# Both gated MLPs' up projections as seven block products per slab, with GpSimd making sums and low parts

## The chip, the cores and the metric

One core of a Trainium2 chip runs the kernel in one launch. The metric is the device time of an execution in microseconds (us). The kernel before takes 1741.75 us, median of 3 runs (1741.56 to 1744.15).

## The reference

Two blocks run one after the other on a sequence of 512 tokens and 1024 channels, in float32. The first has two layers, each a token mixer and a gated MLP; the second has a recurrent and attention mixer and a plain MLP. The change touches the gated MLP of the first block's two layers:

```
def conv_ffn(h, w_up, conv_w, conv_b, w_down):      # h = rms_norm(x, norm2_g), 512 x 1024
    up = h @ w_up                                   # 512 x 5632
    conv = conv_b + padded[:, 0:s_len] * conv_w[0] + ...   # causal, width 3, per channel
    gate, val = jnp.split(conv, 2, axis=-1)         # 2816 each
    return (jax.nn.silu(gate) * val) @ w_down
```

## The kernel before

Every large product is made of three TensorE products in the type fp32r: an operand is split in a high part (ScalarE rounds it, `xh`, `wh`, `ah`) and a low part (the rest, VectorE subtracts, `xl`, `wl`, `al`), and `product` (L573 to L575) issues high x high, high x low, low x high. Weights come as slabs of 128 x 2048 floats (1 MB) in a fixed order through a ring of 3 slots. SyncE loads slab n+3 once TensorE signals `slab_used` for slab n; ScalarE's `high` (L1158) rounds it into `wh`; VectorE's `low_slab` (L1873) writes the rest over the raw slab; `slab_split` tells TensorE. Each engine follows one order written out by hand, with semaphores between them.

A gated MLP works in 11 groups j of 256 gate and 256 value channels: two up slabs and one down slab each. `up` multiplies an up slab with all 8 tiles of x (channels x 512 tokens) into two PSUM banks, 48 products of 512 columns. The tokens aren't normalised before: `scale_up` (L2073) multiplies the result by 1/rms into `upb`. ScalarE makes the first convolution tap (`conv_tap`, L1387), VectorE the other two (`conv_middle` L2079, `conv_first` L2086), ScalarE SiLU (L1397), VectorE the product (`gate`, L2098), ScalarE its high part (L1406), VectorE its low part (`gate_low`, L2103). `down` of group j-1 follows on TensorE behind `up` of group j: 8 output groups o, each 6 products of 512 columns, through 3 banks; VectorE's `add_down` (L2116) adds each to x (layer 0) or to the turned copy `yt` (layer 1), and output group o waits for the add of o-3. In between VectorE multiplies and sums one adaLN slab of the second block per group (`ada_sum`, L1861), which ScalarE's queue loads (L1349). TensorE's order in the loop, two groups per pass:

```
up(j, n, (MLP0 + 2) % RING)
down(it * 2 + v, v, n + 2, (MLP0 + 4) % RING)
```

GpSimd makes the low part of three slabs in the second block (`low`, L558), and nothing else.

## Time and profile before

| | us |
|---|---|
| median of 3 runs | 1741.75 |
| profiled execution | 1741.62 |
| its span, first to last instruction | 1739.8 |
| TensorE busy | 1724.3 (99%) |
| VectorE busy | 1266.6 (73%) |
| ScalarE busy | 769.2 (44%) |
| GpSimd busy | 14.0 (1%) |

In the profile PE is TensorE's matmuls, PEld its weight loads, DVE VectorE, ACT ScalarE, POOL GpSimd, SP SyncE. L573 is line 573 of the kernel. The granted TensorE clock is 0.999 of full speed on average. Durations of matmuls include their way through the array, so they overlap; the distance between two starts is what one costs.

### The profile page before, as it was taken

The numbers are of one execution on the slowest core, as the hardware profiler recorded it, in microseconds if no ns is written. First come the engines' busy times: TensorE is split into PE (matmuls) and PEld (weight loads), VectorE is DVE, ScalarE is ACT, GpSimd is POOL, SyncE is SP. The second block draws the span as 40 slices with busy tenths as digits, with TensorE's granted clock in tenths as the row PEclk, the third lists the DMA queues.
The fourth block names the chain that finished last, engine by engine and source line by source line (L and its number), as shares of the span: only waits on it lengthen the run. The fifth ranks groups of instructions, "written<-read, shape, count | busy, mean of one in ns | idle before, by whom it ended". The sixth has DMA issues, their size and how long they took to land.

```text
span 1739.8 us, 22776 instructions
## 1 busy us (share of the span) xinstructions
PE 1724.3 (99%) x8652; PEld 1403.2 (81%) x8652; DVE 1266.6 (73%) x1788; ACT 769.2 (44%) x1053; POOL 14.0 (1%) x7
## 2 busy tenths in 40 slices
PE   9999999999999999999999999999999999999998
PEld 8896888888888989688888888888766788888886
DVE  6377786776777646878678688766589568777778
ACT  6424442333333523344233233355798474454442
POOL 0000000000000000000000000000000200000000
PEclk9999999999999999999999999999999999999999
DMA  8330334333333233043433433353410233222321
GB/s 291 122 119 27 121 121 145 121 121 132 134 121 121 97 99 120 25 144 110 145 121 121 145 121 121 121 175 122 120 37 2 73 100 112 104 97 97 113 105 49
DMA packets 33352, 195.27 MB, mean 112 GB/s; under 512 B 5760, under 2 KB 7168, under 8 KB 11264
## 3 DMA queue, kind: packets, MB, share of 16 engines
q1 hardware_dynamic: 24656, 156.77, 26.3%
q10 hardware_dynamic: 8624, 37.49, 6.6%
q8 instruction: 50, 0.82, 0.2%
q14 instruction: 22, 0.18, 0.0%
HBM read 187.43 MB, written 2.11 MB: 109 GB/s over the span
## 4 chain that ended last, share of the span: by engine, by line
PE 94%; DVE 3%; issue 1%; ACT 1%; DMA 1%; SPq 0%; DVEq 0%; ACTq 0%; PEldq 0%
PE ps L573 29%; PE ps L574 29%; PE ps L575 29%; PE ps L714 1%; PE ps L728 1%; PE ps L974 1%; PE ps L956 1%; PE ps L992 1%; PE ps L631 1%; DMA raw<-in_weights 1%; DVE acc L2612 1%; PE ps L736 0%; PE ps L892 0%; DMA x<-in_xin 0%; DVE pb L2396 0%
## 5 line engine op out<-in xcount | busy, mean ns | idle before, releaser
L573 PE MATMUL ps<-xh,wh 128*128 128x512 f32 x1440 | 565.1, 392 | 2.3 <-DVE xl L1837 1.8
L574 PE MATMUL ps<-xl,wh 128*128 128x512 f32 x1440 | 560.6, 389 | 0.0
L575 PE MATMUL ps<-xh,wl 128*128 128x512 f32 x1440 | 560.6, 389 | 0.0
L1158 ACT ACTIVATE wh<-raw 128x2048 fp32r<-128x2048 f32 x128 | 244.5, 1913 | 309.2 <-DMA raw<-in_weights 304.5
L573 PEld LDWEIGHTS ps<-xh,wh 128*128 128x128 f32 x1440 | 270.5, 188 | 63.3 <-issue 6.7
L1873 DVE TENSOR_TENSOR wl<-raw,wh 128x2048 fp32r<-128x2048 f32 x110 | 251.5, 2287 | 96.1 <-ACT wh L1158 96.1
L574 PEld LDWEIGHTS ps<-xl,wh 128*128 128x128 f32 x1440 | 270.6, 188 | 56.7 <-issue 1.2
L575 PEld LDWEIGHTS ps<-xh,wl 128*128 128x128 f32 x1440 | 270.4, 188 | 56.8
L1387 ACT ACTIVATE cv<-upb,prm 128x512 f32<-128x512 f32 x88 | 67.0, 809 | 223.5 <-DVE upb L2073 223.5
L1861 DVE CUSTOM_DVE_ANT_0 adab<-adab,crow 128x1024 f32<-128x1024 f32 x44 | 52.2, 1223 | 128.4 <-DMA adab<-in_ada 128.4
L573 PE MATMUL ps<-wh,xh 128*128 128x256 f32 (+1 forms) x352 | 108.3, 308 | 0.0
L575 PE MATMUL ps<-wh,xl 128*128 128x256 f32 (+1 forms) x352 | 106.5, 302 | 0.0
L574 PE MATMUL ps<-wl,xh 128*128 128x256 f32 (+1 forms) x352 | 106.4, 302 | 0.0
L574 PE MATMUL ps<-w2l,a2h 128*128 128x512 f32 x196 | 76.3, 389 | 0.0
L575 PE MATMUL ps<-w2h,a2l 128*128 128x512 f32 x196 | 76.3, 389 | 0.0
L573 PE MATMUL ps<-w2h,a2h 128*128 128x512 f32 x196 | 76.3, 389 | 0.0
L2079 DVE SCALAR_TENSOR_TENSOR cv<-upb,prm,cv 128x511 f32<-128x511 f32 x88 | 64.5, 748 | 15.1 <-ACT cv L1387 15.1
L573 PE MATMUL ps<-wh,ah 128*128 128x512 f32 x176 | 69.3, 394 | 1.7 <-DVE yt L2116 1.7
L573 PEld LDWEIGHTS ps<-wh,xh 128*128 128x128 f32 x352 | 67.2, 191 | 4.7 <-issue 2.0
L574 PEld LDWEIGHTS ps<-wl,xh 128*128 128x128 f32 x352 | 67.3, 191 | 3.3 <-issue 0.7
L573 PE MATMUL ps<-ah,wh 128*128 128x512 f32 x176 | 69.5, 395 | 0.0
L575 PE MATMUL ps<-ah,wl 128*128 128x512 f32 x176 | 69.4, 394 | 0.0
(323 smaller groups left out, 2471.0 us busy)
## 6 DMA issues: line engine op xcount, KB each, us to landing
raw<-in_weights SPq DMA_DIRECT2D x129, 1024.0 KB, 4.9
adab<-in_ada ACTq DMA_DIRECT2D x22, 1024.0 KB, 4.8
both<-in_weights SPq DMA_DIRECT2D x7, 2048.0 KB, 7.6
t<-in_cst ACTq DMA_DIRECT2D x1, 3200.0 KB, 10.2
x<-in_xin SPq DMA_DIRECT2D x8, 256.0 KB, 5.8
turned<-q ACTq DMA_DIRECT2D x8, 256.0 KB, 4.1
turned<-k ACTq DMA_DIRECT2D x8, 256.0 KB, 4.2
adab_tail<-in_ada ACTq DMA_DIRECT2D x2, 1024.0 KB, 10.6
```

Of the source, the lines that this page charges most:

```text
L573: pe.matmul(out, w_hi, m_hi, start=start, stop=False)
L574: pe.matmul(out, w_hi, m_lo, start=False, stop=False)
L575: return pe.matmul(out, w_lo, m_hi, start=False, stop=stop)
L631: return pe.matmul(ps[:, kt, tokens(t)], x[:, NT * (kt // 4) + t, (kt % 4) * P:(kt % 4 + 1) * P], rstd[:, tokens(t)], start=True, stop=True)
L714: last = pe.matmul(ps[:, s_banks[j][hh], s_cols[j]:s_cols[j] + w], k[h, p, j * P:(j + 1) * P], q[h, p, j * P:S], start=True, stop=True)
L728: last = pe.matmul(ps[h, 2, j * P:S], vr[:, j, p * P + HD * hh:p * P + HD * hh + HD], sT[:, p % 2, hh, soffs[j]:soffs[j] + w], start=(j == ...
L956: last = pe.matmul(ps[:, 2 * ((U + 1) % 2) + g, at:at + w], q2[h, r, i * P:(i + 1) * P], ksw[h, b, 0:w], start=True, stop=True)
L1158: act.activation(wh[:, s, :], raw[:, s, :], ACT.Copy).then_inc(hi_made, 1)
L1387: act.activation(cv[:, r, :], upb[:, r, :], ACT.Identity, bias=col(c + 3), scale=col(c + 2)).then_inc(cv_init, 1)
L1861: ins = dve.tensor_tensor_reduce(out=buf[:, m, :], in0=buf[:, m, :], in1=crow[:, :], scale=1.0, scalar=0.0, op0=ALU.mult, op1=ALU.add, acc ...
L1873: dve.tensor_tensor(wl[:, s, :], raw[:, s, :], wh[:, s, :].bitcast(F32), ALU.subtract).then_inc(done, 1)
L2079: dve.scalar_tensor_tensor(cv[:, r, 1:S], upb[:, r, 0:S - 1], col(c0 + (r * 4 + 1)), cv[:, r, 1:S], ALU.mult, ALU.add).then_inc(conv_mid, 1)
```

## The change

Groups 0 and 1 of each MLP stay as they are. Nine groups (j = 2 to 10, `SEVENS` = 18 slabs per layer) compute an up slab in another way. The 1024 x 256 weight slab is cut in 2 x 2 blocks of 512 x 128 (`slab7` stores its four quarters side by side), the tokens in 2 x 2 blocks of 512 channels x 256 tokens, and instead of eight block products `seven` makes seven, from four sums of weight blocks and four of token blocks (Strassen's scheme as Winograd arranged it). A block product is 4 x 3 products of 256 columns. VectorE joins them in 5 adds per slab into `upb`; there is no `scale_up` any more, because VectorE normalises the tokens once per layer, in 8 instructions (`normalise_tokens`), in the arena of the mixer's tables for layer 0 and in x itself for layer 1. ScalarE rounds the seven token blocks once per layer (`bh`, over xh), their rests are made by VectorE (5) and GpSimd (2). GpSimd also makes the four sums of the token blocks once per layer, and, for each up slab, the four sums of weight blocks (`slab_sums`, 512 columns each) and the rests of three of them (`slab_sums_low`, 1536 columns), and for all groups but the last the rest of the down slab and the rests of the gated activations. VectorE keeps the rests of the four blocks that lie in the slab (`blocks_low`, same size as `low_slab`). The mixer's tables, which the arena held, are loaded a second time for layer 1. The core of the diff:

```diff
+PLAIN = 2
+SEVENS = 2 * (NG - PLAIN)
+QUARTER = SLABW // 4
+S4, A11, A12, A22 = range(4)
+S1, S2, S3 = range(4, 7)
+B11, B21, T2, T1, T3, B22, T4 = range(7)
+ONCE, TWICE = 16, 32
...
+        xn0 = at("xn0", [P, KT, S], F32, arena)
+        xn0l = at("xn0l", [P, KT, S], F32R, arena)
+        xn1l = at("xn1l", [P, KT, S], F32R, x_at)
+        tsum = at("tsum", [P, 3, 4, GRP], F32, arena + 16384)
+        tsuml = at("tsuml", [P, 3, 4, GRP], F32R, arena + 16384)
+        bh = at("bh", [P, 7, 4, GRP], F32R, xh_at)
+        wsh = at("wsh", [P, 2, 3, QUARTER], F32R, arena + 28672)
+        wss = at("wss", [P, 2, 3, QUARTER], F32, va_at + 16384)
+        wsl = at("wsl", [P, 2, 3, QUARTER], F32R, va_at + 16384)
+        zc = at("zc", [P, 2, GRP], F32, q_at + 36864)
...
+        def x_block(l, q, kt=None, low=False):
+            if q in (T1, T2, T3):
+                t = (tsuml if low else tsum)[:, (T1, T2, T3).index(q), :, :]
+                return t if kt is None else t[:, kt, :]
+            k, t = {B11: (0, 0), T4: (0, 1), B21: (1, 0), B22: (1, 1)}[q]
+            src = ((xn1l if l else xn0l) if low else normalised(l))[:, 4 * k:4 * k + 4, t * GRP:(t + 1) * GRP]
+            return src if kt is None else src[:, kt, :]
...
+        ONE_BANK, FIVE_BANK, THREE_BANK, SIX_BANK = (0, 7), (1, 0), (2, 1), 3
...
+            def down_slab_low(i, n):
+                pool.wait_ge(hi_made, n + 1)
+                pool.tensor_tensor(wl[:, 1, :], raw[:, 1, :], wh[:, 1, :].bitcast(F32), ALU.subtract).then_inc(down_low, 1)
+            def slab_sums(m, w, s, third):
+                pool.wait_ge(raw_loaded[s], third * 16 + 16)
+                a21, a11, a12, a22 = (quarter(raw, s, i) for i in range(4))
+                pool.tensor_tensor(wss[:, w, 0, :], a21, a22, ALU.add).then_inc(sum_made, 1)
+                pool.tensor_tensor(wss[:, w, 2, :], a11, a21, ALU.subtract).then_inc(sum_made, 1)
+                pool.wait_ge(sum_made, m * 4 + (TWICE + 1))
+                pool.tensor_tensor(wss[:, w, 1, :], wss[:, w, 0, :], a11, ALU.subtract).then_inc(sum_made, 1)
+                pool.wait_ge(sum_made, m * 4 + (TWICE + 3))
+                pool.tensor_tensor(a21, a12, wss[:, w, 1, :], ALU.subtract).then_inc(sum_made, 1)
+            def slab_sums_low(m, w):
+                pool.wait_ge(sum_high, m + (TWICE + 1))
+                pool.tensor_tensor(wsl[:, w, :, :], wss[:, w, :, :], wsh[:, w, :, :].bitcast(F32), ALU.subtract).then_inc(sum_low, 1)
+            def gate_low(l, j, par):
+                for r in range(2):
+                    pool.wait_ge(ah_ready, l * 2 * NG + j * 2 + r + 1)
+                    pool.tensor_tensor(al[:, par, r, :], ab[:, r, :], ah[:, par, r, :].bitcast(F32), ALU.subtract).then_inc(act_split, 1)
+            def token_sums(l):
+                b12 = x_block(l, T4)
+                pool.wait_ge(xn_ready, ONCE + (l + 1) * KT)
+                pool.tensor_tensor(x_block(l, T1), b12, x_block(l, B11), ALU.subtract).then_inc(t_made, 1)
+                pool.tensor_tensor(x_block(l, T3), x_block(l, B22), b12, ALU.subtract).then_inc(t_made, 1)
+                pool.wait_ge(t_made, ONCE + l * 4 + 2)
+                pool.tensor_tensor(x_block(l, T2), x_block(l, B22), x_block(l, T1), ALU.subtract).then_inc(t_made, 1)
+                pool.wait_ge(t_made, ONCE + l * 4 + 3)
+                pool.tensor_tensor(b12, x_block(l, B21), x_block(l, T2), ALU.subtract).then_inc(t_made, 1)
+            def token_low(l, q):
+                pool.wait_ge(t_high, ONCE + l * 7 + q + 1)
+                pool.tensor_tensor(x_block(l, q, low=True), x_block(l, q), bh[:, q, :, :].bitcast(F32), ALU.subtract).then_inc(side_low, 1)
+            for l in range(LAYERS):
+                n0, n3, m0 = l * LAYER_SLABS, l * (LAYER_SLABS // RING), l * SEVENS
+                down_slab_low(l * (NG - 1), n0 + MLP0 + 4)
+                token_sums(l)
+                slab_sums(m0, 0, 2, n3 + 4 + PLAIN)
+                slab_sums_low(m0, 0)
+                slab_sums(m0 + 1, 1, 0, n3 + 5 + PLAIN)
+                token_low(l, T3)
+                token_low(l, B22)
+                with pool.Fori(0, (NG - 1 - PLAIN) // 2) as it:
+                    for v in range(2):
+                        m, third = it * 4 + (m0 + 2 * v), it * 2 + (n3 + PLAIN + v)
+                        slab_sums_low(m + 1, 1)
+                        down_slab_low(it * 2 + (l * (NG - 1) + PLAIN + v - 1), it * 6 + (n0 + 16 + 3 * (PLAIN + v)))
+                        gate_low(l, it * 2 + (PLAIN + v - 1), (PLAIN + v - 1) % 2)
+                        slab_sums(m + 2, 0, 2, third + 5)
+                        slab_sums_low(m + 2, 0)
+                        slab_sums(m + 3, 1, 0, third + 6)
+                slab_sums_low(m0 + SEVENS - 1, 1)
+                down_slab_low(l * (NG - 1) + NG - 2, n0 + LAYER_SLABS - 2)
+                gate_low(l, NG - 2, (NG - 2) % 2)
...
+                def seven(m, w, n, s):
+                    def operands(a, low):
+                        if a >= S1:
+                            return (wsl if low else wsh)[:, w, a - S1, :]
+                        return quarter(wl if low else wh, s, a)
+                    def block_product(out, a, q):
+                        if w == 0 and q not in (T3, B22):
+                            pe.wait_ge(t_low, ONCE + l * 5 + (B11, B21, T2, T1, T4).index(q) + 1)
+                        elif w == 0:
+                            pe.wait_ge(side_low, SIDE + l * 2 + (T3, B22).index(q) + 1)
+                        hi, lo = operands(a, False), operands(a, True)
+                        for kt in range(4):
+                            c = slice(kt * P, (kt + 1) * P)
+                            last = product(out, hi[:, c], lo[:, c], bh[:, q, kt, :], x_block(l, q, kt, low=True),
+                                           kt == 0, kt == 3)
+                        return last
+                    def joined_before(count):
+                        if w:
+                            pe.wait_ge(half_joined, m * 5 + (TWICE - 5 + count))
+                    pe.wait_ge(slab_split, n + 1)
+                    if w == 0:
+                        pe.wait_ge(half_joined, m * 5 + TWICE)
+                    block_product(half_bank(ONE_BANK[w], 0), A11, B11)
+                    block_product(half_bank(ONE_BANK[w], 1), A12, B21).then_inc(part_done, 1)
+                    joined_before(1)
+                    pe.wait_ge(sum_low, m + (TWICE + 1))
+                    block_product(half_bank(SIX_BANK, w), S2, T2).then_inc(part_done, 1)
+                    joined_before(2)
+                    block_product(half_bank(FIVE_BANK[w], 0), S1, T1)
+                    block_product(half_bank(FIVE_BANK[w], 1), S3, T3).then_inc(part_done, 1)
+                    joined_before(4)
+                    block_product(half_bank(THREE_BANK[w], 0), S4, B22)
+                    block_product(half_bank(THREE_BANK[w], 1), A22, T4).then_inc(slab_used, 1)
...
+                up(1, n0 + MLP0 + 2, (MLP0 + 2) % RING)
+                down(0, 0, n0 + MLP0 + 4, (MLP0 + 4) % RING)
+                past(pe, up_scaled, (l + 1) * 4 * PLAIN)
+                with pe.Fori(0, (NG - 1 - PLAIN) // 2) as it:
                     for v in range(2):
-                        j = it * 2 + (1 + v)
-                        n = it * 6 + (n0 + MLP0 + 2 + 3 * v)
-                        up(j, n, (MLP0 + 2) % RING)
-                        down(it * 2 + v, v, n + 2, (MLP0 + 4) % RING)
+                        n, m = it * 6 + (n0 + 14 + 3 * (PLAIN + v)), it * 4 + (l * SEVENS + 2 * v)
+                        seven(m, 0, n, 2)
+                        seven(m + 1, 1, n + 1, 0)
+                        down(it * 2 + (PLAIN + v - 1), (PLAIN + v - 1) % 2, n + 2, 1)
+                seven((l + 1) * SEVENS - 2, 0, n0 + LAYER_SLABS - 4, 2)
+                seven((l + 1) * SEVENS - 1, 1, n0 + LAYER_SLABS - 3, 0)
...
+                def seven_step(j, par, m, n, third, last=False):
+                    keep_first(m, 0, j)
+                    sums_high(m + 1, 1)
+                    ada_load(l * NG + j)
+                    high(n + 2, 1, third + 5)
+                    high_gate(j - 1, par)
+                    joined_taps(m, 0, j)
+                    keep_first(m + 1, 1, j)
+                    if last:
+                        high(n + 3, 2, third + 5)
+                    else:
+                        blocks_high(2, third + 5)
+                    silu(j)
+                    if not last:
+                        fourth_high(m + 2, 2)
+                        sums_high(m + 2, 0)
+                    joined_taps(m + 1, 1, j)
+                    if last:
+                        high(n + 4, 0, third + 6)
+                    else:
+                        blocks_high(0, third + 6)
+                        fourth_high(m + 3, 0)
...
+                    for dst, src in ((t1[:, :], cst1[:, C1_KEEP:C1_N]), (bsb[:, :, :], bsb_in), (bw[:, :, :], bw_in), (ws[:, :, :], wsT)):
+                        act.dma_start(dst, src).then_inc(tables_loaded, 16)
...
+                def normalise_tokens():
+                    for kt in range(KT):
+                        dve.scalar_tensor_tensor(normalised(l)[:, kt, :], x[:, kt, :], col(l * PC_LN + (PC_L + 16 + kt)), rstd[:, :],
+                                                 ALU.mult, ALU.mult).then_inc(xn_ready, 1)
...
+                def early_joins(m, w):
+                    dve.wait_ge(half_kept, m + (TWICE + 1))
+                    dve.wait_ge(part_done, m * 3 + (TWICE + 2))
+                    dve.tensor_tensor(zc[:, w, :], up_quarters(w, 0), half_bank(SIX_BANK, w), ALU.add).then_inc(half_joined, 1)
+                    dve.wait_ge(half_joined, m * 5 + (TWICE + 1))
+                    dve.tensor_tensor(up_quarters(w, 0), up_quarters(w, 0), half_bank(ONE_BANK[w], 1), ALU.add).then_inc(half_joined, 1)
+                def middle_joins(m, w):
+                    dve.wait_ge(part_done, m * 3 + (TWICE + 3))
+                    dve.tensor_tensor(up_quarters(w, 1, 2).rearrange("p (h t) -> p h t", h=2),
+                                      bank(FIVE_BANK[w]).rearrange("p (h t) -> p h t", h=2),
+                                      zc[:, w:w + 1, :].broadcast_to((P, 2, GRP)), ALU.add).then_inc(half_joined, 1)
+                    dve.wait_ge(half_joined, m * 5 + (TWICE + 3))
+                    dve.tensor_tensor(up_quarters(w, 3), up_quarters(w, 2), half_bank(FIVE_BANK[w], 0), ALU.add).then_inc(half_joined, 1)
+                def late_join(m, w, n):
+                    dve.wait_ge(slab_used, n + 1 + RING)
+                    dve.wait_ge(half_joined, m * 5 + (TWICE + 4))
+                    dve.tensor_tensor(up_quarters(w, 1, 2), up_quarters(w, 1, 2), bank(THREE_BANK[w]), ALU.add).then_inc(half_joined, 1)
+                def seven_step(j, m, n):
+                    each(conv_middle, j - 1, (2, 3))
+                    each(conv_first, j - 1, (2, 3))
+                    early_joins(m, 0)
+                    each(gate, j - 1, (0, 1))
+                    middle_joins(m, 0)
+                    late_join(m, 0, n)
+                    ada_sum(l * NG + j, adab, l * NG + j + 1)
+                    early_joins(m + 1, 1)
+                    each(conv_middle, j, (0, 1))
+                    conv_first(j, 0)
+                    middle_joins(m + 1, 1)
+                    conv_first(j, 1)
+                    late_join(m + 1, 1, n + 1)
...
+                def first_blocks(o):
+                    if o == 0:
+                        token_low(B11)
+                    elif o == 1:
+                        token_low(B21)
+                    elif o == 3:
+                        token_low(T2)
+                    elif o == 5:
+                        token_low(T1)
+                    elif o == 7:
+                        token_low(T4)
+                blocks_low(n0 + MLP0 + 5, 2, 1)
+                add_down(0, n0 + MLP0 + 4, first_blocks)
+                ada_keep(l * NG + 1)
+                blocks_low(n0 + MLP0 + 6, 0, 2)
...
-                        low_slab(n + 1, MLP0 % RING)
-                        ada_sum(l * NG + j, adab, l * NG + j + 1)
-                        low_slab(n + 2, (MLP0 + 1) % RING)
-                        for r in range(2):
-                            scale_up(j, n, r)
-                        each(conv_middle, j, (0, 1))
-                        each(conv_first, j, (0, 1))
-                        low_slab(n + 3, (MLP0 + 2) % RING)
-                        for r in range(2, 4):
-                            scale_up(j, n, r)
-                        add_down(it * 2 + v, n + 2, values_part, early=(6, 7))
+                        j, n = it * 2 + (PLAIN + v), it * 6 + (n0 + 14 + 3 * (PLAIN + v))
+                        seven_step(j, it * 4 + (l * SEVENS + 2 * v), n)
+                        def next_blocks(o):
+                            if o == 1:
+                                blocks_low(n + 3, 2, 1)
+                        add_down(it * 2 + (PLAIN + v - 1), n + 2, next_blocks)
                         ada_keep(l * NG + j)
+                        blocks_low(n + 4, 0, 2)
...
+def slab7(w):
+    b = w.reshape(2, 4, P, 2, P)
+    return np.concatenate([b[k, :, :, m, :].transpose(1, 0, 2).reshape(P, QUARTER) for m, k in ((1, 0), (0, 0), (0, 1), (1, 1))], 1)
```

## Rows read from the trace of the kernel before

**Rows 1.** The page, part 1: busy time, share, instructions of each engine

```profile
PE 1724.3 (99%) x8652; PEld 1403.2 (81%) x8652; DVE 1266.6 (73%) x1788; ACT 769.2 (44%) x1053; POOL 14.0 (1%) x7
```

**Rows 2.** The page, part 4: the chain that ended last, share by engine

```profile
PE 94%; DVE 3%; issue 1%; ACT 1%; DMA 1%; SPq 0%; DVEq 0%; ACTq 0%; PEldq 0%
```

**Rows 3.** Busy time by stretch; columns in the first line

```profile
core 0: us, PE busy (x) PEld busy (x) DVE busy (x) ACT busy (x) POOL busy (x), PEclk, DMA share, GB/s
250.00:558.00 308.00, 308.00 (x1346) 251.95 (x1345) 233.03 (x305) 104.68 (x104) 0.00 (x0) 1.00 0.37 126
```

**Rows 4.** Timeline of TensorE, one step; start us, us, instruction

```profile
294.50 0.39 PE L573 MATMUL ps<-xh,wh 128*128 128x512 f32 x1
...
305.40 0.39 PE L573 MATMUL ps<-xh,wh 128*128 128x512 f32 x1
...
316.28 0.39 PE L573 MATMUL ps<-ah,wh 128*128 128x512 f32 x1
...
327.48 0.39 PE L573 MATMUL ps<-xh,wh 128*128 128x512 f32 x1
```

**Rows 5.** Timeline of TensorE, a token-major slab of the mixer

```profile
20.31 0.28 PE L573 MATMUL ps<-wh,xh 128*128 128x256 f32 x1
...
26.43 0.28 PE L573 MATMUL ps<-wh,xh 128*128 128x256 f32 x1
```

**Rows 6.** Timeline of VectorE in the same step

```profile
305.04 1.23 DVE L1861 CUSTOM_DVE_ANT_0 adab<-adab,crow 128x1024 f32<-128x1024 f32 x1 [7.17 <-DMA adab<-in_ada]
...
307.34 2.29 DVE L1873 TENSOR_TENSOR wl<-raw,wh 128x2048 fp32r<-128x2048 f32 x1
309.54 1.28 DVE L2073 TENSOR_TENSOR upb<-ps,rstd 128x512 f32<-128x512 f32 x2
311.46 1.44 DVE L2079 SCALAR_TENSOR_TENSOR cv<-upb,prm,cv 128x511 f32<-128x511 f32 x2 [0.63 <-ACT cv L1387]
312.81 1.41 DVE L2086 SCALAR_TENSOR_TENSOR cv<-upb,prm,cv 128x510 f32<-128x510 f32 x2
```

**Rows 7.** Groups by line, 300 to 1120 us; busy us, mean ns, idle before

```profile
L2116 DVE TENSOR_TENSOR x<-x,ps 128x512 f32<-128x512 f32 x72 | 49.2, 685 | 3.4
...
L2098 DVE TENSOR_TENSOR ab<-cv 128x512 f32<-128x512 f32 x38 | 25.9, 685 | 0.0
...
L1824 DVE RECIPROCAL rstd<-std 128x512 f32<-128x512 f32 x2 | 6.7, 3352 | 6.9 <-ACT std L1176 6.9
...
L1982 DVE TENSOR_TENSOR sT<-ps,t 128x256 f32<-128x256 f32 x4 | 1.7, 414 | 0.0
...
L1158 ACT ACTIVATE wh<-raw 128x2048 fp32r<-128x2048 f32 x72 | 137.7, 1913 | 204.3 <-DMA raw<-in_weights 204.3
L1387 ACT ACTIVATE cv<-upb,prm 128x512 f32<-128x512 f32 x76 | 57.9, 810 | 197.3 <-DVE upb L2073 197.3
L1406 ACT ACTIVATE ah<-ab 128x512 fp32r<-128x512 f32 x38 | 23.9, 631 | 37.5 <-DVE ab L2098 37.5
```

**Rows 8.** Timeline of GpSimd's slab rests, and of VectorE beside them

```profile
1259.71 4.55 POOL L558 TENSOR_TENSOR wl<-raw,wh 128x2048 fp32r<-128x2048 f32 x1 [1259.26 <-ACT wh L1158]
1371.19 4.60 POOL L558 TENSOR_TENSOR wl<-raw,wh 128x2048 fp32r<-128x2048 f32 x1 [106.93 <-ACT wh L1158]
1378.15 4.60 POOL L558 TENSOR_TENSOR wl<-raw,wh 128x2048 fp32r<-128x2048 f32 x1 [2.36 <-ACT wh L1158]
...
1262.70 0.55 DVE L2358 CUSTOM_DVE_ANT_0 pb<-ps,tsl 128x384 f32<-128x384 f32 x1 [4.31 <-issue]
...
1263.66 3.35 DVE L2413 RECIPROCAL rstd<-std 128x512 f32<-128x512 f32 x1
...
1382.75 1.89 DVE L2440 TENSOR_TENSOR yg<-ps,g1row 128x512 f32<-128x512 f32 x3 [12.79 <-ACT sqb L1654]
```

**Rows 9.** The page, part 6: DMA issues; KB each, median us to landing

```profile
raw<-in_weights SPq DMA_DIRECT2D x129, 1024.0 KB, 4.9
...
t<-in_cst ACTq DMA_DIRECT2D x1, 3200.0 KB, 10.2
```

181 lines of the change are left out of this document (135 added, 46 removed).

## The prediction, made before the change was timed

> **What bounds the kernel now.** I read the page's busy shares first: TensorE 99%, VectorE 73%, ScalarE 44%, GpSimd 1% [rows 1]. The chain that ended last says the same: 94% of the span on TensorE, 3% on VectorE [rows 2]. So inside the MLPs only shorter TensorE work helps, as long as nothing else becomes later. In 308 us of the first MLP VectorE is busy 233 us, GpSimd not at all [rows 3]. The TensorE timeline gives the step of one group j: 294.50 to 305.40 to 316.28 are the two up slabs (10.9 us each, 48 products of 512 columns, 0.227 us apart), to 327.48 the down slab (11.2); a step takes 33.0 us [rows 4]. Durations in the trace's columns overlap, so I use distances between starts everywhere.
>
> **The change, TensorE.** A token-major slab shows 256-column products: 20.31 to 26.43 is 51 of them, 0.120 us apart, though each loads its own weights [rows 5]. A seven-product slab has 7 x 4 x 3 = 84 such products: 10.1 us instead of 10.9. That saves 0.8 us in each of 9 groups x 2 slabs x 2 layers = 36 slabs: 29 us. It is all the change can gain. An unstalled step becomes 2 x 10.1 + 11.2 = 31.4 us; events below are timed from the start of its first up slab, the down slab starting at 20.2.
>
> **VectorE.** From its timeline: 2048 columns of two SBUF tensors 2.20 us, adaLN sum 2.30 for both halves, a 512-column convolution tap 0.68 [rows 6]; products of 512 columns and adds from PSUM 0.6, and 256 columns from PSUM about 0.34, both taken as the listed means less the 0.08 by which starts lie closer [rows 7]. Before, a step holds 3 slab rests (6.6), the sum (2.3), 4 scalings (2.4), 8 taps (5.4), 2 gates and 2 gate rests (2.4), 8 adds (4.8): 23.9 us. After: 2 slab rests (4.4), sum 2.3, 8 taps 5.4, 2 gates 1.2, 8 adds 4.8, joins 2 x (0.34 + 0.34 + 0.6 + 0.34 + 0.6) = 4.4: 22.5 us. That fits in 31.4.
>
> **ScalarE.** 2048 columns take 1.9 us, a tap 0.75, a 512-column copy 0.6 [rows 7]. Three slabs plus two times three quarter-slab sums make 5.7 + 2.9, with taps 3.0, SiLU 1.2, gate copies 1.2 and two kept quarters (0.8) 14.8 us. It fits.
>
> **GpSimd.** Its three slab rests of 2048 columns took 4.6 us each [rows 8]: 2.24 ns a column, twice VectorE's. A step now gives it, per up slab, four quarter sums (4.6) and the sums' rests (1536 columns, 3.45), then the down slab's rest (4.6) and two gate rests (2.3): 10,240 columns, 22.9 us. Fixed costs of short instructions aren't shown; 13 instructions at 0 to 0.1 us add 0 to 1.3.
>
> **Does the step close if engines don't disturb one another?** The tightest path is the next first slab. Its slot is free at 10.1; a load lands 5 to 6 us later (4.9 median from issue [rows 9]), so at 16. GpSimd's sums end at 20.7, the rounded fourth quarter follows at 21.3 (0.5), VectorE's rest, queued behind down add 1, at 23.5 to 25.7. Product group 5 of the down slab (27.0) waits for add 2: 26.3. Some 0.7 us is left there, 2 to 3 us elsewhere; the sums' rest is due at 33.9 and done at 26.5; down rests at 12.9 and gate rests at 15.2 are due at 20.2. So the step closes at 31.4.
>
> **Start of each MLP.** Count from its first up slab, as before: groups 0 and 1 end at 21.8 and 43.5, down slab 0 runs to 54.4. VectorE now scales x 8 times (8 x 0.68 = 5.5), done at 29. The down slab's load can start at 21.8, takes 5.3 and is rounded at 29 [rows 7, 9]. GpSimd then does its rest 4.6, token sums 4 x 2.3, block sums 4.6: 47.4. Only then come the fourth quarter (0.5), VectorE's rest (2.2), and behind it down add 0 at 51; TensorE's group 3 wanted it at 47.6. With the five token rests of 1.15 us between the adds, the first seven-product slab starts at 59 instead of 54: 5 us lost per layer, 10 in all. Behind nothing it would be 0, with no overlap of token sums at all 9, so 0 to 18 for both. The tables under the reused arena are loaded again (3.2 MB took 10.2 us to land [rows 9]) at the layer boundary, where a slot has 21.8 us for load, rounding and rest (9.1): nothing, 3 us at most.
>
> **The two instructions that have never met.** All this holds GpSimd's 22.9 us beside VectorE's. No row shows a GpSimd instruction beside a VectorE one that reads two SBUF tensors. At 1371.19 and 1378.15 VectorE was idle (its next work, at 1382.75, had waited 12.8 us); at 1259.71 to 1264.26 it read at most one SBUF tensor, and its reciprocal kept its usual 3.35 us [rows 7, 8]. After the change nearly all GpSimd work meets such pairs: slab rests 4.4, taps 5.4, gates 1.2, sum 2.3 = 13.3 us per step. Joins and down adds read one operand from PSUM. The cost is bounded by nothing (they pass each other: 31.4 us) and by full exclusion: 22.9 + 13.3 = 36.2 us of work that can't overlap, already more than the 33.0 of before. The measured pair that is nearest, GpSimd beside a one-operand VectorE instruction, cost nothing; but it lacks just the second read. GpSimd reads two SBUF tensors at less than half VectorE's pace, so both engines would want a second stream all the time. I take exclusion as likelier than not; it is a choice, the rows leave it open.
>
> The Trainium skill ("SBUF — State Buffer", Who interferes with whom) states that a VectorE instruction with two SBUF inputs contends with a GpSimd instruction that reads SBUF, the later one blocking for the whole instruction. By that page the sum would be the slow case below; without it the fast one. No row here shows it, and it strengthens my choice.
>
> **Forecast: exclusion (0.60).** The step by hand: VectorE gets its turn whenever GpSimd's instruction ends, and keeps it through a run. From 4.0 its second slab rest and four taps run to 9.0; GpSimd's sum rest 12.5; gates 13.7; down rest 18.3; adaLN sum 20.6; first gate rest 21.8; three taps 23.9; second gate rest 25.1. The down slab wanted that at 20.2: TensorE waits 4.9 us. Last tap 25.8; block sums 30.4; rounding 30.9; slab rest 33.1; add 2 33.7, wanted at 31.9: another 1.8. The down slab ends at 37.8 while sum rest and block sums run to 41, which is 3.3 of the next step, where I began. Thus 36.2 plus two handovers through ScalarE of 0.6 is 37.4, 37.8 by the longer walk, and I take 38 for fixed costs. If the two engines alternate instruction by instruction, the same walk gives 41. Sixteen such steps (the last of each layer makes no sums and stays at 33): 16 x 5.0 = 80 us. At the start of the MLP GpSimd's 18.4 us and VectorE's 10.1 us of paired work (eight taps, gates, gate rests, adaLN sum) follow one another from 29: the sums end at 57.6 instead of 47.4, add 0 at 61, and token rests waiting for sum rests put the first seven-product slab at 72: 18 us per layer, 36. Sum against the profiled execution: 1741.6 (span 1739.8 and 1.8 around it; the runs' median is 1741.75, so no correction) + 80 + 36 = **1858 us**. Its own range: 16 x 3.2 + 20 = 71 above, so 1813, up to 16 x 8 + 46 = 174, so 1915; a lower granted clock after waits of 5 us, which the trace never has, would push up inside that.
>
> **Rival 1, other sign: no interference (0.30).** GpSimd and VectorE pass each other, the step closes at 31.4: 1741.6 - 29 + 10 = **1723 us**; 1714 to 1731 with start losses of 1 to 18. For it: each engine alone fits with 8 us to spare, and GpSimd beside one-operand work was undisturbed [rows 8]. The deciding point is whether paired work overlaps by more than 3.2 of its 13.3 us (36.2 less 33.0): above that the sign turns.
>
> **Rival 2: partial sharing (0.10).** Both engines go on but GpSimd slows while VectorE reads two tensors. If half of the 13.3 us is lost, 29.6 us of shared work still fits, but the 0.7 us of room before add 2 and the block sums' path don't: GpSimd's sums come about 2 us later, the step is 33 and the start costs 10 us per layer: 1741.6 + 0 + 20 = **1762 us**; between 1735 and 1813.
>
> **How the numbers follow.** Slower: exclusion 0.60 and most of partial sharing, 0.07, make 0.67. Faster: 0.30 and 0.01. Within 0.2% (3.5 us, about what a measurement of this kernel can tell from no change): 0.02. The cases have opposite signs, so the range must reach from the fast one to the slow one: 1716 to 1915 leaves out some of the fast tail and the worst walks. The likeliest case's own range is 1813 to 1915.
>
> **What the profile after would show.** Matmuls of 256 columns 0.12 us apart and 10.1 us a slab in any case. Exclusion: VectorE taps, gates and slab rests much longer than 0.7 and 2.3 us beside GpSimd, or idle that ends with GpSimd, and down adds from PSUM at their old 0.69; steps of 37 to 41 us; TensorE waiting for act_split and the down adds, busy near 85% in the MLPs. GpSimd rests stretched above 4.6 us would be the same thing from the other side. No interference: taps at 0.75, steps of 31.4, TensorE idle only in the first 60 us of each MLP. I am wrong if the step is under 33 us, or if it is long with paired instructions at their old durations: then the cause is a queue (GpSimd's order, or ScalarE's rounding behind SiLU), not the two engines' reads.

## The result and the profile after

Changed kernel: 1924.63 us, median of 4 runs (1924.0 to 1925.59). Before, beside it: 1741.97 us (1741.56 to 1744.15). The ratio is 1.1046, 95% interval 1.1027 to 1.1065: 183 us slower. Forecast were 1858 us for the likeliest case and 1716 to 1915 as the range. The sign was right, the time lies 10 us beyond the range.

The page of the profiled execution, busy shares and chain:

```profile
span 1922.2 us, 26092 instructions
...
PE 1755.5 (91%) x9948; PEld 1483.4 (77%) x9948; DVE 1514.1 (79%) x1867; ACT 842.6 (44%) x1175; POOL 588.5 (31%) x255
...
PE 53%; issue 20%; POOL 17%; DVE 8%; ACT 2%; DMA 0%; POOLq 0%; SPq 0%; DVEq 0%; PEldq 0%; ACTq 0%
```

TensorE had 94% of the chain before [rows 2] and has 53% now; GpSimd, absent there, has 17%. No engine is fully busy: that points to engines that wait for one another. What TensorE waited for (us in total, times, longest):

```profile
PE ps L692 <- DVE zc L2403: 77.1, 18, 5.9
PE ps L692 <- DVE yt L2379: 32.8, 17, 12.9
PE ps L692 <- DVE x L2379: 32.6, 16, 13.1
PE ps L692 <- DVE wl L2133: 9.0, 2, 4.5
```

The first is once per seven-product step: the third block product of the second up slab needs the bank half that the first join of the first slab (`zc`, L2403) reads. The next two are down adds, 13 us of each at the start of an MLP. The last is at each MLP's end.

VectorE and GpSimd in 300 to 560 us, forms apart (count, then busy, mean ns, then idle before and its releaser):

```profile
L2342 DVE SCALAR_TENSOR_TENSOR cv<-upb,prm,cv 128x511 f32<-128x511 f32 x26 | 72.8, 2838 | 0.0
L2379 DVE TENSOR_TENSOR x<-x,ps 128x512 f32<-128x512 f32 x51 | 33.3, 684 | 11.9 <-PE ps L694 11.9
L2121 DVE CUSTOM_DVE_ANT_0 adab<-adab,crow 128x1024 f32<-128x1024 f32 x14 | 30.2, 2190 | 0.0
L2397 DVE TENSOR_TENSOR wl<-raw,wh 128x2048 fp32r<-128x2048 f32 x13 | 29.8, 2293 | 20.1 <-ACT wh L1583 20.1
L2349 DVE SCALAR_TENSOR_TENSOR cv<-upb,prm,cv 128x510 f32<-128x510 f32 x26 | 26.0, 1019 | 0.0
```
```profile
L633 POOL TENSOR_TENSOR wsl<-wss,wsh 128x1536 fp32r<-128x1536 f32 x13 | 53.9, 4150 | 52.4 <-ACT wsh L1588 52.4
L617 POOL TENSOR_TENSOR wl<-raw,wh 128x2048 fp32r<-128x2048 f32 x6 | 30.0, 5005 | 0.0
L623 POOL TENSOR_TENSOR wss<-raw 128x512 f32<-128x512 f32 x13 | 24.0, 1847 | 0.0
```

The taps of L2342 take 2838 ns where one took some 750; adaLN halves 2190 where the trace before had 1223. The adds from PSUM keep 684 ns [rows 7]. The slab rests keep 2293 because GpSimd has nothing to do, or waits, while they run. One step, VectorE first, then GpSimd (start, duration):

```profile
406.62 2.29 DVE L2397 TENSOR_TENSOR wl<-raw,wh 128x2048 fp32r<-128x2048 f32 x1 [3.36 <-ACT wh L1583]
408.83 8.96 DVE L2342 SCALAR_TENSOR_TENSOR cv<-upb,prm,cv 128x511 f32<-128x511 f32 x2
417.71 1.40 DVE L2349 SCALAR_TENSOR_TENSOR cv<-upb,prm,cv 128x510 f32<-128x510 f32 x2
419.03 0.41 DVE L2403 TENSOR_TENSOR zc<-upb,ps 128x256 f32<-128x256 f32 x1
```
```profile
266.14 3.47 POOL L633 TENSOR_TENSOR wsl<-wss,wsh 128x1536 fp32r<-128x1536 f32 x1 [5.31 <-ACT wsh L1588]
...
404.56 1.28 POOL L628 TENSOR_TENSOR raw<-raw,wss 128x512 f32<-128x512 f32 x1
408.24 4.04 POOL L633 TENSOR_TENSOR wsl<-wss,wsh 128x1536 fp32r<-128x1536 f32 x1 [2.39 <-ACT wsh L1588]
412.24 5.00 POOL L617 TENSOR_TENSOR wl<-raw,wh 128x2048 fp32r<-128x2048 f32 x1
421.24 2.52 POOL L639 TENSOR_TENSOR al<-ab,ah 128x512 fp32r<-128x512 f32 x2 [4.00 <-ACT ah L1573]
...
437.10 4.25 POOL L633 TENSOR_TENSOR wsl<-wss,wsh 128x1536 fp32r<-128x1536 f32 x1 [5.43 <-ACT wsh L1588]
```

Read them together. GpSimd's 1536-column rest is recorded from 408.24, but VectorE's slab rest runs to 408.91; undisturbed it takes 3.47 (the row at 266.14), so it began when VectorE ended. The first tap stands behind it until 412.3, runs, and then GpSimd's 2048-column rest, recorded from 412.24, takes its turn until 417.24; only then comes the second tap. Two taps: 8.96 us. **Durations in these rows include the wait for the other engine**, and here the engines take turns, one instruction each. The seams overlap a little: at 4.55 us undisturbed [rows 8] the 2048-column rest began at 412.7, some 0.4 us into a tap of 0.7 (an estimate from these rows). TensorE, at the same place:

```profile
402.29 0.28 PE L692 MATMUL ps<-bh,wh 128*128 128x256 f32 x1
...
414.95 0.28 PE L694 MATMUL ps<-bh,wl 128*128 128x256 f32 x1
419.57 0.57 PE L692 MATMUL ps<-bh,wsh 128*128 128x256 f32 x1 [4.34 <-DVE zc L2403]
```

Distances between `ada_keep` (L2128 after, L1868 before), which each group issues once, split the loss; before they were 25.7 and 26.2 for the first interval of a layer, then 32.98 and 32.75. Layer 0 after: first one 9.0 late, then 36.26, 39.6, seven of 40.64 to 41.6, and 37.69. Layer 1 the same within 0.3. Both layers:

- starts (9.0 and 9.1 before the first, 10.6 and 10.3 in the first interval): 39.0 us
- sixteen seven-product steps (39.6 or 39.3, then 40.7 each but one of 41.6 per layer, against 33.0 and 32.75): 124.6 us
- the last step of each layer, 37.7 and 37.8 against 33.0 and 32.75: 9.8 us
- from there to the end of each MLP: 6.0 and 3.0, 9.0 us

Together 182.4 us, the difference of the spans (1922.2 and 1739.8).

### The profile page after: what moved, and what is told of

It reads as the page before. It is cut to its first block, busy times and chain, and to the rows that moved or that the text cites. A ratio compares the mean times of both kernels' runs of the same rounds, so it can differ in the third digit from the quotient of the medians.

```text
span 1922.2 us, 26092 instructions
## 1 busy us (share of the span) xinstructions
PE 1755.5 (91%) x9948; PEld 1483.4 (77%) x9948; DVE 1514.1 (79%) x1867; ACT 842.6 (44%) x1175; POOL 588.5 (31%) x255
## 4 chain that ended last, share of the span: by engine, by line
PE 53%; issue 20%; POOL 17%; DVE 8%; ACT 2%; DMA 0%; POOLq 0%; SPq 0%; DVEq 0%; PEldq 0%; ACTq 0%
PE ps L692 15%; PE ps L694 15%; PE ps L693 15%; POOL wl L617 4%; POOL wss L623 3%; POOL wss L626 3%; POOL raw L628 2%; POOL wsl L633 2%; DVE cv L2342 2%; POOL al L639 2%; DVE adab L2121 1%; PE ps L833 1%; PE ps L847 1%; PE ps L1143 1%; DVE al L2366 1%
## 5 line engine op out<-in xcount | busy, mean ns | idle before, releaser
L692 PE MATMUL ps<-xh,wh 128*128 128x512 f32 x864 | 340.4, 394 | 2.3 <-DVE xl L2097 1.8
L694 PE MATMUL ps<-xh,wl 128*128 128x512 f32 x864 | 336.5, 389 | 0.0
L693 PE MATMUL ps<-xl,wh 128*128 128x512 f32 x864 | 336.3, 389 | 0.0
L2342 DVE SCALAR_TENSOR_TENSOR cv<-upb,prm,cv 128x511 f32<-128x511 f32 x88 | 219.4, 2529 | 2.9 <-ACT cv L1555 2.9
L692 PE MATMUL ps<-bh,wsh 128*128 128x256 f32 x432 | 141.5, 328 | 77.1 <-DVE zc L2403 77.1
L633 POOL TENSOR_TENSOR wsl<-wss,wsh 128x1536 fp32r<-128x1536 f32 x36 | 148.7, 4129 | 135.8 <-ACT wsh L1588 135.8
L692 PE MATMUL ps<-bh,wh 128*128 128x256 f32 x576 | 162.1, 281 | 1.4 <-DVE wl L2397 1.4
L694 PE MATMUL ps<-bh,wl 128*128 128x256 f32 x576 | 162.2, 282 | 0.0
L693 PE MATMUL ps<-tsuml,wsh 128*128 128x256 f32 x432 | 139.4, 323 | 0.0
L694 PE MATMUL ps<-bh,wsl 128*128 128x256 f32 x432 | 137.1, 317 | 0.0
```

Of the source, the lines that this page charges most:

```text
L633: pool.tensor_tensor(wsl[:, w, :, :], wss[:, w, :, :], wsh[:, w, :, :].bitcast(F32), ALU.subtract).then_inc(sum_low, 1)
L692: pe.matmul(out, w_hi, m_hi, start=start, stop=False)
L693: pe.matmul(out, w_hi, m_lo, start=False, stop=False)
L694: return pe.matmul(out, w_lo, m_hi, start=False, stop=stop)
L2342: dve.scalar_tensor_tensor(cv[:, r, 1:S], upb[:, r, 0:S - 1], col(c0 + (r * 4 + 1)), cv[:, r, 1:S], ALU.mult, ALU.add).then_inc(conv_mid, 1)
```

## Experiments

Unless said otherwise a variant is of the changed kernel and ran once, beside the kernel before at 1741.0 to 1742.5 us; differences under 2 us are read as none. Step lengths are distances between `ada_keep`; where one length is given it is that of the steady steps, and a mean is over the sixteen steps of both layers, 40.65 us in the changed kernel.

**1. GpSimd writes, but hardly reads.** It computes the first 8 columns of each row and writes zeros over the rest; so it leaves out nearly all arithmetic of the sums and rests. All its additions and subtractions in the MLPs are changed like the one shown:

```diff
+                pool.tensor_tensor(out[few], a[few], b[few], op)
+                return pool.memset(out[rest].bitcast(F32), 0.0)
...
-                pool.tensor_tensor(wl[:, 1, :], raw[:, 1, :], wh[:, 1, :].bitcast(F32), ALU.subtract).then_inc(down_low, 1)
+                mostly_zero(wl[:, 1, :], raw[:, 1, :], wh[:, 1, :].bitcast(F32), ALU.subtract).then_inc(down_low, 1)
```


> Edit of the changed kernel: each GpSimd subtraction or addition does only its first 8 columns of each row, and writes zeros over the rest, so GpSimd reads almost nothing from SBUF; every wait and signal stays. Left out: the block sums, the low parts and the token sums are therefore wrong beyond those columns. Theory (GpSimd's two-operand instructions and VectorE's instructions with two SBUF operands exclude each other, one instruction at a time): VectorE's taps fall back to 0.75 us each, the step closes at 31.4 to 32 us instead of 40.7, the start of each MLP loses 0 to 5 us, total 1712 to 1735. Rival (the hand-written order of the queues, ScalarE's rounding behind SiLU and VectorE's joins, makes the long step, not the reads): some of GpSimd's time is gone but the step stays above 35 us, total above 1780.

Measured: 1720.53 us, steps of 31.03. In 300 to 560 us:

```profile
L2404 DVE TENSOR_TENSOR wl<-raw,wh 128x2048 fp32r<-128x2048 f32 x14 | 32.0, 2285 | 0.0
...
L2349 DVE SCALAR_TENSOR_TENSOR cv<-upb,prm,cv 128x511 f32<-128x511 f32 x34 | 24.0, 745 | 0.0
```

With GpSimd's reads and most of its time gone, taps are back at 745 ns, and the gain of TensorE is there. But it made GpSimd faster too (504 columns written in 0.52 us), so it doesn't yet tell reads from mere work. Runs 2 to 5 do: they put work that serves nothing on GpSimd in the kernel **before**, where it is otherwise idle.

**2 to 4. Thirteen instructions of 512 columns beside the taps, in the kernel before.** They start when a group's second quarter is scaled. They differ in what they read:

```diff
+                    past(pool, up_scaled, l * 4 * NG + j * 4 + 2)
+                    for i in range(13):
+                        pool.wait_ge(lru_exp, done[0])
+                        pool.tensor_tensor(spare[:, :], spare[:, :], spare[:, :], ALU.add).then_inc(lru_exp, 1)
```
In the second the instruction is `tensor_scalar(spare, spare, 1.0, None, ALU.mult)`, in the third `memset(spare, 0.0)`.

> Edit of the kernel before: GpSimd makes 13 additions of 512 columns with two SBUF operands (1.28 us each alone) in each of 18 groups, now from the third scaling of the group's first half on, so that they meet the taps, slab rests and gates. Theory (exclusion, one instruction each in turn): taps and gates beside them go from 0.75 and 0.69 to between 1.3 and 2.1 us, slab rests to at most 3.6, adds and scalings from PSUM stay at 0.69 us; 16.7 us of GpSimd and some 13 us of VectorE's paired work follow one another, the step may grow from 33 to between 33 and 40, total 1745 to 1860. Rival (no interference): 1741 and unchanged durations.

> As the run with two reads, at the same places, but each GpSimd instruction multiplies one SBUF operand by a constant: one read, one write. If any GpSimd instruction that reads SBUF takes turns with VectorE's two-operand instructions, taps beside it are stretched by up to this instruction's own duration, which I expect at 0.5 to 0.9 us; total 1741 to 1800. If only two-operand GpSimd instructions did, the taps would stay at 0.75 us.

> As the run with two reads, at the same places, but each GpSimd instruction is a memset: it only writes (0.53 us each). If the shared thing is the read side, taps, gates and rests keep their durations and the time stays at 1741 within 3 us; if writes collide as well, taps grow by up to 0.5 us.

Measured: 1772.98 us with two reads, 1742.01 with one, 1741.95 with none. One row of taps from each, in that order, 300 to 560 us:

```profile
L2093 DVE SCALAR_TENSOR_TENSOR cv<-upb,prm,cv 128x511 f32<-128x511 f32 x30 | 31.2, 1058 | 5.0 <-ACT cv L1400 5.0
```
```profile
L2093 DVE SCALAR_TENSOR_TENSOR cv<-upb,prm,cv 128x511 f32<-128x511 f32 x32 | 26.4, 839 | 5.0 <-ACT cv L1400 5.0
```
```profile
L2093 DVE SCALAR_TENSOR_TENSOR cv<-upb,prm,cv 128x511 f32<-128x511 f32 x32 | 23.5, 748 | 5.0 <-ACT cv L1400 5.0
```

In the same windows the adds from PSUM were 674, 675 and 685 ns, the scalings 678, 680 and 683. The writing instructions (311.49 to 319.04 in the group looked at) had four taps and a slab rest beside them and stretched neither. So what stretches the taps is a GpSimd instruction that **reads** SBUF, one operand or two, beside a VectorE instruction that reads two SBUF operands. The Trainium skill ("SBUF — State Buffer", Who interferes with whom) states that such a VectorE instruction contends with a GpSimd instruction that reads SBUF, not with one that only writes it; the trace agrees (1058 and 839 ns against 748). One read stretches the taps less, though GpSimd's instruction was recorded as longer (1689 ns against 1440 with two reads); how long it holds VectorE off isn't its whole duration, and wasn't measured. It costs no time: VectorE had the room. Two reads brought steps of 34.3 to 34.7.

**5. Ten two-operand adds, from the fourth down add on, in the kernel before.**

```diff
+                    past(pool, ffn_added, l * 8 * NG + (j - 1) * 8 + (4 if j > 1 else 1))
+                    for i in range(10):
```


> Edit of the kernel before: GpSimd, idle there, makes ten additions of 512 columns with two SBUF operands in each group of both MLPs (18 groups, from the fourth down add of the group on), on a buffer that nobody else uses. Nothing of the kernel's own work changes. Theory (exclusion): GpSimd's 12.8 us per group stretch VectorE's taps, slab rests, gates and adaLN sums beside them to about double (a tap 1.5 to 2 us), adds from PSUM stay at 0.69; VectorE had 9 us to spare per step, so the time grows by 5 to 80 us. Rival (no interference): the same time within 3 us and taps at 0.75.

Measured: 1741.65 us, a miss. Gate rests went from 684 to 1159 ns and gates from 685 to 799, but taps kept their 748: the adds met few of them and fell into idle time of VectorE (up to 5.9 us there). Contention is real here and free: it costs nothing while the engine has a reserve.

**6. ScalarE rounds the next block sums before the SiLU.**

```diff
-                    silu(j)
                     if not last:
...
                         sums_high(m + 2, 0)
+                    silu(j)
```


> Edit of the changed kernel: ScalarE rounds the fourth quarter and the three weight sums of the next first slab before the SiLU of the group instead of behind it. Nothing is left out. In the trace of the changed kernel GpSimd is idle for 5.4 us there in each step (431.7 to 437.1), while SiLU waits for a tap that VectorE makes late. Theory (exclusion sets the step through the chain GpSimd sums, rounding, GpSimd's rests, GpSimd sums): the idle time falls to about 2.2 us, the step from 40.7 to 37.5 to 39, total 1870 to 1900. Rival (VectorE's and GpSimd's work together fills the step whatever the order): within 10 us of 1924.6.

Measured: 1884.83 us, steady steps of 38.0, 2.7 less (the first of each layer grew, to 42.6 and 40.8, so the mean is 38.5). TensorE's wait for the joins nearly vanished:

```profile
PE ps L692 <- DVE zc L2403: 9.6, 2, 5.4
```

The rows of after show GpSimd idle for 5.43 us behind `wsh` (437.10): time in which nobody used the turn.

**7. GpSimd's long rests cut into 512 columns.**

```diff
-                pool.tensor_tensor(wl[:, 1, :], raw[:, 1, :], wh[:, 1, :].bitcast(F32), ALU.subtract).then_inc(down_low, 1)
+                for c in range(4):
+                    last = pool.tensor_tensor(quarter(wl, 1, c), quarter(raw, 1, c), quarter(wh, 1, c).bitcast(F32), ALU.subtract)
+                last.then_inc(down_low, 1)
```
(and three pieces for `wsl`)

> Edit of the changed kernel: GpSimd's instructions of 2048 and 1536 columns cut into pieces of 512 (1.28 us each alone), same work, same order. Theory (the two engines take turns instruction by instruction): a tap beside them waits at most one piece, so the mean of the middle tap falls from 2.53 us to 1.5 to 2.0, and VectorE gets through its four taps earlier; the step falls from 40.7 to between 38.5 and 40.5, total 1890 to 1922. Rival (VectorE is held until GpSimd has nothing more to do): the middle tap stays at 2.5 us and the time at 1924.

Measured: 1882.2 us, better than my theory expected, steps of 35.6 to 40.7, mean 38.8. Taps of L2342 fell from 2838 to 1552 ns, those of L2349 rose from 1019 to 1504. Short instructions cost GpSimd more in all and still won: a VectorE instruction now waits for 1.28 us of GpSimd's at a time, not for 3.47 or 4.55.

**8. Both edits.**

> Both edits that shortened the step of the changed kernel, together: ScalarE rounds the next block sums before the SiLU (alone: steps of 38.0 us, 1884.8 us in all) and GpSimd's rests of 2048 and 1536 columns are cut into instructions of 512 (alone: steps of 35.6 to 40.2, mean 38.4, 1882.2 us). Theory (two engines that may not read SBUF at the same time): the step cannot fall below the sum of the work that excludes itself, some 25 us on GpSimd in short pieces (19 of 1.28) and 13.3 us of paired work on VectorE; so the two gains don't add, steps stay at 37.5 to 39 us and the time is 1870 to 1890 us. Rival (the time was lost in the order of the work and in turns waited for, not in exclusion): the gains add, 2.7 and 2.3 us off 40.7, steps of 35.7 us and 1835 to 1850 us.

Measured: 1883.56 us, steps of 35.5 to 40.7, mean 38.7: the gains don't add. (The expectation took 38.4 for run 7 alone; over all sixteen steps it is 38.8.) The expectation's count should have been 20 pieces: 20 x 1.28 = 25.6 of GpSimd and 13.3 of paired VectorE work are 38.9. The mean stands 0.2 below that sum; the overlap at the seams and the 13.3 aren't known better than that. Each edit alone had already come to the bound that exclusion sets (run 7: the same 38.9, measured 38.8; run 6: 10 x 1.28 + 2 x 3.47 + 4.55 = 24.3, + 13.3 = 37.6, measured 38.0 in the steady steps).

**9. Gate rests back on VectorE** (`gate_low` from GpSimd's program to a place between the middle joins and the late join).

```diff
-                        gate_low(l, it * 2 + (PLAIN + v - 1), (PLAIN + v - 1) % 2)
...
                     middle_joins(m, 0)
+                    for r in range(2):
+                        gate_low(j - 1, par, r)
```


> Edit of the changed kernel: the low parts of the gated activations go back from GpSimd to VectorE, behind the middle joins. Nothing is left out. Theory (exclusion): 2.5 us of GpSimd's work per step become 1.2 us of VectorE's, so 1.3 us less that can't overlap; the step falls by 1 to 2 us, total 1890 to 1910. Rival (VectorE is the bound by its own amount of work): the step grows by 1.2 us, total about 1945.

Measured: 1925.96 us, steps 40.87; both theories missed. TensorE's wait only moved:

```profile
PE ps L690 <- DVE zc L2401: 111.8, 18, 7.7
```

GpSimd, spared the gate rests, makes its block sums earlier, where they stretch the second two taps in front of the join (3.41 us, were 1.40). Then it idles longer before the next sums' rest, 13.36 us where it was 5.43:

```profile
437.46 4.24 POOL L633 TENSOR_TENSOR wsl<-wss,wsh 128x1536 fp32r<-128x1536 f32 x1 [13.36 <-ACT wsh L1586]
```

It waits for ScalarE's rounding behind the SiLU, the place that run 6 moved. Less work that can't overlap gained nothing while that order held; whether both edits together gain wasn't tried.

**10 to 13. Less and less on GpSimd.** Run 10 takes sums and gate rests from it; run 11 also cuts the down rest and moves the second slab's rest; run 12 leaves only the down rest; run 13 leaves nothing. VectorE does it instead, where its order allows (the last line of the cut only in runs 12 and 13):

```diff
-                token_sums(l)
-                slab_sums(m0, 0, 2, n3 + 4 + PLAIN)
...
+                        slab_sums(m + 2, 0, 2, third + 5)
                         add_down(it * 2 + (PLAIN + v - 1), n + 2, next_blocks)
                         ada_keep(l * NG + j)
+                        slab_sums_low(m + 2, 0)
```


> Edit of the changed kernel: block sums, token sums and the gated activations' low parts on VectorE; GpSimd keeps the rests of the weight sums, of two token blocks and of the down slabs. Nothing is left out. By durations from the profiles: VectorE 28.5 us per step, of it 19.3 with two SBUF operands; GpSimd 11.5; together 30.8 that can't overlap, under the 31.0 of TensorE. Theory (exclusion, plus VectorE's waits in its own order): the step falls from 40.7 to 32 to 35, the start of each MLP loses 3 to 10 us instead of 19; total 1730 to 1790. Rival (VectorE's amount of work never mattered and the order of queues does): stays above 1850.

> Edit of the run with the sums on VectorE, where two taps took 8.99 us behind a GpSimd rest of 1536 and one of 2048 columns: the rest of the second slab's sums goes to VectorE too (in front of the late join), the down slab's rest on GpSimd is cut into four pieces. VectorE 30.1 us per step, GpSimd 8.5, together 29.5 that can't overlap. Theory (long GpSimd instructions in front of the taps made that step long, not the sum of work): the step falls from 38.4 to 33 to 35.5, total 1765 to 1830. Rival (VectorE's own order with the block sums in it is the cause): 38 or more.

> As the run before, with all rests of sums and of token blocks on VectorE; GpSimd keeps only the down slab's rest, in four pieces. VectorE 31.8 us per step. Theory: VectorE becomes the bound, the step is 32 to 34.5, total 1745 to 1800; against the run before it gains if exclusion still costs more than 1.7 us there. Nothing is left out.

> The seven products with nothing on GpSimd in the MLPs: sums and all rests on VectorE, 34.0 us of its work per step by the durations in the profiles. No interference is possible; the step is VectorE's own 34 to 35.5, taps 0.75, total 1765 to 1815. It is slower than the kernel before by VectorE's amount of work alone, and faster than the change by more than 100 us.

Measured: 1889.97, 1832.47, 1831.54 and 1830.22 us, steady steps of 38.4, about 35.2, 35.3 and 34.8 to 36.3. All four miss their range. In run 10 the two long rests still stood before the taps, though GpSimd had half its work:

```profile
401.82 4.05 POOL L633 TENSOR_TENSOR wsl<-wss,wsh 128x1536 fp32r<-128x1536 f32 x1 [5.27 <-ACT wsh L1581]
405.83 5.03 POOL L617 TENSOR_TENSOR wl<-raw,wh 128x2048 fp32r<-128x2048 f32 x1
```
```profile
402.41 8.99 DVE L2335 SCALAR_TENSOR_TENSOR cv<-upb,prm,cv 128x511 f32<-128x511 f32 x2
```

The same 9 us for two taps as in the changed kernel: halving GpSimd's work left this place as it was. Run 11 changed its order, length and amount together and took 3.2 us off the step, so their shares aren't separated. Run 13 shows the other bound. Busy times in 300 to 560 us (PE, weight loads, DVE, ACT, POOL, granted clock):

```profile
300.00:560.00 260.00, 235.49 (x1564) 213.57 (x1563) 254.00 (x354) 108.71 (x126) 0.00 (x0) 0.98 0.33 117
```

VectorE is busy 254 of 260 us with taps at their 747 ns. With nothing on GpSimd the step is VectorE's own work, still 2 to 3 us above 33. The expectation had left out the starts, which lose about 14 us per layer, and the first seven-product step of each layer, 40.7 and 40.4.

**14. The last down slab's rest made earlier.** The change had moved `low_slab(n + 3, 2)` of each MLP's last group behind the eight down adds before it.

```diff
                         gate(j, o - 4)
+                        if o == 4:
+                            low_slab(n + 3, 2)
...
                 ada_keep(l * NG + j)
-                low_slab(n + 3, 2)
```


> The changed kernel with one line moved: VectorE makes the rest of each MLP's last down slab behind the fifth down add of the slab before, not behind all eight. The changed kernel's TensorE waits 4.4 us there in each layer. Theory (the queue on VectorE: from the last join on it is busy without a break, with 4 taps, 2 gates, 2 gate rests, 8 adds and then this rest): the wait goes over to the gate rests, which now come 2.2 us later, and shrinks by some 2 us per layer: 1919 to 1923 us. Rival (the place of the rest alone makes the wait): both waits go, 1914 to 1917 us. No effect would be 1924 to 1925.5.

Measured: 1919.58 us, inside the theory's range. TensorE's wait goes over from `wl` to the down adds, 3.2 us in layer 0 where it was 4.4; the theory had named the gate rests as its new place. In the changed kernel VectorE's queue from the last join to this rest has one idle stretch in layer 0, of 0.74 us, so what is put earlier pushes back nearly all behind it. 5 of the 9 us came back.

No variant that does the whole computation came below the kernel before; 1830 us is the best.

## Why the prediction was right and wrong

**TensorE's part: right.** Products of 256 columns 0.12 apart, and 31.03 us a step in run 1 (forecast 31.4). Run 1 as a whole, 1720.5, is what rival 1 gave (1723).

**The mechanism: right, and shown.** The choice that the prediction called open, exclusion between a two-operand VectorE instruction and a GpSimd instruction that reads, is what runs 1 to 4 show: taps stretched, down adds as they were. Rival 1 falls with the steps of 40.7, rival 2 (partial sharing) with the timeline, in which one engine stands until the other's instruction ends (but for some 0.3 us at the seams), and with run 8, whose two gains stop at the sum of the work. Work that cannot overlap, 36.2 us in the prediction, is 37.6 by measured durations: 512 columns took GpSimd 1.28 us, not 1.15, 1536 took 3.47, 2048 took 4.55. That is a fixed cost of some 0.2 us per instruction, where I had put 0 to 0.1.

**The step that failed: "VectorE gets its turn whenever GpSimd's instruction ends, and keeps it through a run."** It gave 37.8 us and I took 38. In the steady step the timeline shows the engines alternating, one instruction each, so that each of the first two taps waits for a long rest. Counted from the start of the first up slab (402.29), the walk has the four taps end at 9.0; they end at 16.8. TensorE's wait comes from there: 4.3 us for the join behind the taps, and 2.0 for down adds. For the gate rests, where the walk had 4.9, it doesn't wait. The same paragraph's other walk, "if the two engines alternate instruction by instruction", gave 41; measured are 40.7. I had that number and used it as the end of the range. But the prediction shows no working for 41, so its closeness may be luck. On sixteen steps: 124.6 us measured, 80 forecast, **44.6 of the 66.6 us by which I missed**. Runs 6 and 7 show what is in the 2.7 us: with the wait behind the SiLU gone, or with GpSimd's instructions short, the mean step falls to 38.5 or 38.8, and run 8 (38.7) that both only lead to the same bound. So 38 was the bound, and the walk to it was not what this order of work achieves.

**"The last of each layer makes no sums and stays at 33": wrong.** It took 37.7: it makes no new sums, but GpSimd's timeline still has a down rest in it (at 615.60, 5.02 us) and the gate rests (at 624.62). 9.8 us for both layers.

**The ends of the MLPs: overlooked.** I priced the diff's move of the last down slab's rest at nothing, without naming it. 9.0 us; run 14 returned 5. TensorE still waits for down adds there (3.2 us in layer 0); what else holds the other 4 isn't settled.

**The starts: right in size.** 36 forecast, 39.0 measured. Rows: 13.1 us of wait for one down add while VectorE's taps, gates and adaLN sum alternate with GpSimd's block sums.

**The clock.** The prediction had a lower granted clock pushing up inside its range. It falls; that it costs little in the steady step is argued from these windows, not shown:

```profile
403.00:415.00 12.00, 12.00 (x104) 12.00 (x102) 8.64 (x5) 4.09 (x4) 9.53 (x5) 1.00 0.60 205
415.00:419.50 4.50, 0.23 (x2) 0.02 (x1) 4.46 (x5) 0.00 (x0) 2.24 (x1) 0.86 0.36 151
419.50:424.00 4.50, 4.43 (x21) 4.43 (x21) 4.43 (x7) 2.10 (x4) 2.76 (x3) 0.50 0.00 0
424.00:428.00 4.00, 4.00 (x31) 4.00 (x31) 3.97 (x7) 2.31 (x3) 4.00 (x2) 0.86 0.00 0
```

After 4.3 us without work TensorE runs at the lower of its two levels (1.2 GHz, the row's 0.50) for 4.5 us and more: 21 products there, where 0.12 apart 37 would go. TensorE's 40.7 us hold 6.3 of waits and so 34.3 of products, where run 1 needs 31.03 in all. But VectorE is busy 99% of the last three windows, so the late products mostly meet an engine that is late anyway. How much the clock costs by itself wasn't separated.

The sum on record and what was measured: starts 36 and 39.0, steps 80 and 124.6, last steps 0 and 9.8, ends 0 and 9.0; 116 and 182.4. The range's upper end allowed 174 for starts and steps, which took 163.6; what carried the time beyond it are the two terms at 0, 18.8 us.

## What to carry to other kernels

Before work is given to an idle GpSimd, add its instructions that read two SBUF operands to VectorE's that do: in these runs the two didn't overlap but for the seams, and if the sum is above the present step, the move loses however idle each engine looks. Walk the order with one instruction per turn as the slow case, and keep GpSimd's instructions short: a tap waited for the whole of the one before it. And for every instruction that a diff moves, name what it now stands behind, the ends of a loop too.

## What the runs showed that I had not expected

- The turn doesn't always alternate. At the start of each MLP VectorE ran four taps and two gates at their usual durations past a GpSimd rest that was already waiting, and let it in only at its first gap (238.13 to 238.23): of 7.93 us 4.55 are work. It is the same in layer 1, and in run 1, where an instruction of 8 columns took 3.56 us there. What decides between this and the alternation at 408 wasn't tried.

```profile
234.67 7.93 POOL L617 TENSOR_TENSOR wl<-raw,wh 128x2048 fp32r<-128x2048 f32 x1 [234.22 <-ACT wh L1327]
```
```profile
234.19 1.41 DVE L2342 SCALAR_TENSOR_TENSOR cv<-upb,prm,cv 128x511 f32<-128x511 f32 x2
235.52 1.41 DVE L2349 SCALAR_TENSOR_TENSOR cv<-upb,prm,cv 128x510 f32<-128x510 f32 x2
236.84 1.29 DVE L2361 TENSOR_TENSOR ab<-cv 128x512 f32<-128x512 f32 x2
238.23 7.72 DVE L2366 TENSOR_TENSOR al<-ab,ah 128x512 fp32r<-128x512 f32 x2
```

- Waits are booked as busy time of the waiting instruction: VectorE's 79% in the page holds taps of 2838 ns of which 750 are work. A busy share is no measure of load when two engines hold each other off; the count times the same form's shortest duration is.
- The tiny one counts too: an instruction of 2 columns (`ada_keep`) took 2.41 us beside GpSimd, against 0.16 alone. It has one tensor operand, so runs 2 to 4 don't cover it. And it isn't held off by reads alone: in run 1, in both layers, it ended with a GpSimd instruction that only writes (second and third row). Why it contends wasn't tried.

```profile
282.13 2.41 DVE L2128 TENSOR_SCALAR mod<-ada_pair 128x2 f32<-128x2 f32 x1
```
```profile
242.40 0.52 DVE L2135 TENSOR_SCALAR mod<-ada_pair 128x2 f32<-128x2 f32 x1
241.10 1.80 POOL L619 MEMSET wl<- 128x2040 f32 x1
```

- Cutting GpSimd's instructions shorter, which costs it some 1.3 us per step in fixed costs, made the kernel 42 us faster than leaving them long (1882.2 against 1924.6).
